# Expert blocks on one Trainium2 core: token rows kept as rounded values and rests, turned in the rounded type through three PSUM banks

## The reference, cut to what matters

```python
xb = h_pad[slot_tok].reshape(n_blocks, MOE_BLOCK, d)      # MOE_BLOCK = 128, d = 1024

def expert_block(args):
    xi, e = args
    return (jax.nn.silu(xi @ w_gate[e]) * (xi @ w_up[e])) @ w_down[e]   # 1024 -> 512 -> 1024

yb = lax.map(expert_block, (xb, block_expert)).reshape(n_blocks * MOE_BLOCK, d)
y = jax.ops.segment_sum(yb * slot_w[:, None].astype(yb.dtype), slot_tok, num_segments=n + 1)
```

## Time and profile before

| what | value |
|---|---|
| median of 3 runs | 4618.35 us (4615.28 to 4619.43) |
| the profiled execution's own time | 4615.54 us |
| its span in the profile | 4613.7 us |
| busy share of the span | PE 86%, PEld 63%, DVE 45%, ACT 34%, POOL 14% |
| mean granted clock of TensorE | 0.915 |
| DMA | 451.03 MB, mean 98 GB/s |

### The profile page before, as it was taken

How to read it: one execution, slowest core, us unless ns; L and a number is a source line. 1 busy time by engine, 2 the same in 40 slices (tenths; PEclk the granted TensorE clock), 3 DMA queues, 4 the chain that set the end, 5 groups by cost and what they waited for, 6 DMA issues and landing times. The chain is left out here.

```text
span 4613.7 us, 42989 instructions
## 1 busy us (share of the span) xinstructions
PE 3988.9 (86%) x16492; PEld 2886.4 (63%) x16492; DVE 2089.2 (45%) x2604; ACT 1548.8 (34%) x2420; POOL 652.5 (14%) x332
## 2 busy tenths in 40 slices
PE   6799789999799799995956899889999854999996
PEld 6587555558587355573735776567777744666664
DVE  0272366652381466722237413223442213666665
ACT  1312245541322354422141335321220112555552
POOL 0021200002021100020100011123333221110111
PEclk6799889998899799987988899999999966999997
DMA  4211100012121112231212111132333233999985
GB/s 157 72 37 39 35 14 28 28 33 82 64 51 35 25 55 60 64 105 46 39 45 45 41 30 14 28 87 73 82 96 71 75 112 111 355 352 356 354 295 218
DMA packets 354838, 451.03 MB, mean 98 GB/s; under 512 B 51981, under 2 KB 227266, under 8 KB 354130
## 3 DMA queue, kind: packets, MB, share of 16 engines
q1 hardware_dynamic: 341986, 423.11, 29.7%
q0 software_dynamic: 12656, 25.26, 1.5%
HBM read 408.39 MB, written 59.31 MB: 101 GB/s over the span
## 5 line engine op out<-in xcount | busy, mean ns | idle before, releaser
L1189 PE MATMUL values<-probs,vp 128*128 128x512 f32 x672 | 348.4, 600 | 12.0 <-issue 6.4
L1277 ACT ACTIVATE probs<-scores 128x512 f32<-128x512 f32 (+1 forms) x336 | 196.0, 583 | 306.3 <-PE scores L213 304.6
L211 PE MATMUL scores<-q_hi,k_rest 97*128 97x512 f32 (+1 forms) x336 | 262.2, 780 | 0.0
L3417 PE MATMUL dp<-h_t,abt 128*128 128x512 f32 x544 | 241.9, 597 | 1.1 <-ACT abt L3466 0.9
L3448 ACT ACTIVATE expert_hi<-wu 128x1024 fp32r<-128x1024 f32 x136 | 144.7, 1064 | 250.4 <-PE gp L213 250.4
L255 POOL TENSOR_TENSOR ring_r<-ring_w,ring_hi 128x1024 fp32r<-128x1024 f32 x44 | 116.7, 2654 | 758.7 <-ACT ring_hi L248 758.7
L1358 DVE TENSOR_REDUCE mx<-made 128x1 f32<-128x640 f32 (+1 forms) x272 | 203.7, 793 | 27.3 <-PE made L1130 26.5
L211 PE MATMUL smb<-x_t_r,merge_w_r 128*128 128x512 f32 x480 | 196.0, 408 | 19.1 <-POOL merge_w_r L2758 16.4
L211 PE MATMUL gates_ps<-x_t_r,ring_r 128*128 128x512 f32 (+1 forms) x560 | 206.2, 368 | 2.9 <-PEq L81 2.9
L779 DVE SCALAR_TENSOR_TENSOR conv_out<-conv_in,vectors,conv_out 128x1295 f32<-128x1295 f32 (+1 forms) x120 | 205.5, 1713 | 4.3
L212 PE MATMUL gates_ps<-h_t_r,ring_hi 128*128 128x512 f32 (+1 forms) x560 | 206.2, 368 | 0.0
(11 more groups left out here) (521 smaller groups left out, 9580.4 us busy)
## 6 DMA issues: line engine op xcount, KB each, us to landing
wg<-in_w_gate SPq DMA_DIRECT2D x34, 2048.0 KB, 9.7
wu<-in_w_up SPq DMA_DIRECT2D x34, 2048.0 KB, 11.0
h_t<-in_w_down SPq DMA_DIRECT2D x34, 2048.0 KB, 9.6
ahead_w<-in_w_ada SPq DMA_DIRECT2D x48, 512.0 KB, 3.9
ring_w<-in_w_in SPq DMA_DIRECT2D x44, 512.0 KB, 4.1
mod_w<-in_w_mod SPq DMA_DIRECT2D x12, 1024.0 KB, 5.3
x_kept<-x_t SPq DMA_DIRECT2D x6, 2048.0 KB, 12.0
ahead_w<-in_w_mod SPq DMA_DIRECT2D x24, 512.0 KB, 3.6
```

What stands on the lines that cost most here:

```text
L211: nc.tensor.matmul(out, lhs[1], rhs[0], start=start, stop=False, **kw)
L1189: nc.tensor.matmul(O[b % 2][:, 0:w], vp[g // 2 % 2][:, kb, g % 2 * VD:g % 2 * VD + P], pr[m % 3][:, 0:w], start=kb == 0, stop=kb == nk - 1 ...
L1277: nc.scalar.activation(pr[m % 3][:, 0:w], S[m % 2][:, 0:w], ACT.Exp, scale=scale).then_inc(s.exped, 1)
L3417: m = nc.tensor.matmul(dp[half][:, :], at[:, j, :], wd[u][:, j, half * 512:(half + 1) * 512], start=j == 0, stop=j == FK - 1)
```

## The change

`turn_out` writes each token row as 2048 values where it was 1024: the 1024 rounded values, then the 1024 rests. ACT's copy out of PSUM goes into a tile of the rounded type, and DVE, which had no part in this stage, subtracts it from the bank (L700 in the new file). A store is 1024 KB. A gather brings both parts of a row, 8 KB where it was 4 KB. `turn_x` has 16 transpositions, with data, identity and result in the rounded type, in four groups: the rounded values of features 0 to 511, their rests, the rounded values of features 512 to 1023, their rests. They go to three banks, so the fourth group takes the first group's bank again. ACT copies banks 0 and 2 to `x_hi`, DVE banks 1 and 0 to `x_rest`; DVE's part is a copy and no longer needs `x_hi`. The first gather buffer moves to a free part of the old h. The rounded identity is made by ACT at the start of the stage.

```diff
@@ turn_out @@
-    with ExitStack() as es, stage(nc, "turned copied out0 out1") as s, nc.Block() as block:
-        rows = [es.enter_context(sbuf(nc, f"to_rows{i}", [P, DK, P], F32)) for i in range(2)]
+    with ExitStack() as es, stage(nc, "turned rounded rest out0 out1") as s, nc.Block() as block:
+        rows = [es.enter_context(sbuf(nc, f"to_rows{i}", [P, 2, DK, P], F32R)) for i in range(2)]
...
                     if n >= 4:
-                        pe.wait_ge(s.copied, n - 3)
+                        pe.wait_ge(s.rest, n - 3)
...
                     act.wait_ge(s.turned, n + 1)
-                    nc.scalar.activation(rows[i % 2][:, 4 * h:4 * h + 4, :], ps[n % 4][:, :, :], ACT.Copy)\
-                        .then_inc(s.copied, 1)
+                    nc.scalar.activation(rows[i % 2][:, 0, 4 * h:4 * h + 4, :], ps[n % 4][:, :, :], ACT.Copy)\
+                        .then_inc(s.rounded, 1)
+
+        @block.vector
+        def _(dve):
+            for i in range(n_tiles):
+                if i >= 2:
+                    dve.wait_ge(stored[i % 2], 16 * (i // 2))
+                for h in range(2):
+                    n = 2 * i + h
+                    dve.wait_ge(s.rounded, n + 1)
+                    nc.vector.tensor_tensor(rows[i % 2][:, 1, 4 * h:4 * h + 4, :], ps[n % 4][:, :, :],
+                                            rows[i % 2][:, 0, 4 * h:4 * h + 4, :].bitcast(F32), ALU.subtract).then_inc(s.rest, 1)
...
-                sp.wait_ge(s.copied, 2 * (i + 1))
-                sp.dma_start(out[i * P:(i + 1) * P, :], rows[i % 2][:, :, :].rearrange("p c t -> p (c t)"))\
-                    .then_inc(stored[i % 2], 16)
+                sp.wait_ge(s.rest, 2 * (i + 1))
+                sp.dma_start(out[i * P:(i + 1) * P, :],
+                             rows[i % 2][:, :, :, :].rearrange("p a c t -> p (a c t)").bitcast(F32)).then_inc(stored[i % 2], 16)
@@ experts: tiles @@
-            xb = two("xb", [P, D])
+            xb1, xb1_r = es.enter_context(sbuf_views(nc, "xb1", [P, 2 * D]))
+            xb = [flat_h[:, 2 * FK * D:2 * FK * D + 2 * D], xb1]
+            xb_r = [k.h_r[:, :, :].rearrange("p a b -> p (a b)")[:, 2 * FK * D:2 * FK * D + 2 * D], xb1_r]
+            ident_r = sb("ident_r", [P, P], F32R)
...
-            xp = [es.enter_context(psum(nc, f"xp{i}", [P, 4, P], F32)) for i in range(2)]
+            xp = [es.enter_context(psum(nc, f"xp{i}", [P, 4, P], F32R)) for i in range(3)]
@@ experts: POOL (fixed blocks; the loop likewise) @@
-                        pool.wait_ge(s.xt_made, 2 * (b - 1))
+                        pool.wait_ge(s.xt_made, 4 * (b - 1))
@@ experts: PE @@
                 def turn_x(b, u):
                     pe.wait_ge(gathered[u], count(b, 8, 16 - 8 * u))
-                    for half in range(2):
-                        if later(b):
-                            pe.wait_ge(s.x_rest, count(b, 2, half - 1))
+                    for n in range(4):
+                        half, part = divmod(n, 2)
+                        if n == 3:
+                            pe.wait_ge(s.x_hi, count(b, 2, 1))
+                        elif later(b):
+                            pe.wait_ge(s.x_hi if n == 2 else s.x_rest, count(b, 2, 0))
                         for q in range(4):
-                            c = 4 * half + q
-                            m = nc.tensor.transpose(xp[half][:, q, :], xb[u][:, c * P:(c + 1) * P], k.ident)
+                            c = part * DK + 4 * half + q
+                            m = nc.tensor.transpose(xp[n % 3][:, q, :], xb_r[u][:, c * P:(c + 1) * P], ident_r[:, :])
                         m.then_inc(s.xt_made, 1)
 
                 def gate_up(b, u):
+                    pe.wait_ge(s.x_hi, count(b, 2, 2))
                     pe.wait_ge(s.x_rest, count(b, 2, 2))
...
+                pe.wait_ge(s.ident_made, 1)
                 turn_x((None, 0), 0)
@@ experts: ACT @@
                 def round_x(b):
                     for half in range(2):
-                        act.wait_ge(s.xt_made, count(b, 2, half + 1))
-                        nc.scalar.activation(x_hi[:, 4 * half:4 * half + 4, :], xp[half][:, :, :], ACT.Copy)\
+                        act.wait_ge(s.xt_made, count(b, 4, 2 * half + 1))
+                        nc.scalar.activation(x_hi[:, 4 * half:4 * half + 4, :], xp[2 * half][:, :, :], ACT.Copy)\
                             .then_inc(s.x_hi, 1)
...
+                nc.scalar.activation(ident_r[:, :], k.ident, ACT.Copy).then_inc(s.ident_made, 1)
                 round_x((None, 0))
@@ experts: DVE @@
                 def rest_x(b):
                     for half in range(2):
-                        dve.wait_ge(s.x_hi, count(b, 2, half + 1))
+                        dve.wait_ge(s.xt_made, count(b, 4, 2 * half + 2))
                         chunks = slice(4 * half, 4 * half + 4)
-                        nc.vector.tensor_tensor(x_rest[:, chunks, :], xp[half][:, :, :], x_hi[:, chunks, :].bitcast(F32),
-                                                ALU.subtract).then_inc(s.x_rest, 1)
+                        nc.vector.tensor_copy(x_rest[:, chunks, :], xp[1 - half][:, :, :]).then_inc(s.x_rest, 1)
@@ second_block @@
-    r.rows = nc.dram_tensor("token_rows", [SEQ, D], F32, kind="Internal").ap()
+    r.rows = nc.dram_tensor("token_rows", [SEQ, 2 * D], F32, kind="Internal").ap()
```

More of the change, by code:

```diff
@@ L3264, in turns_of @@
             return eng.value_load(r.block_expert[0:1, LOOPED:LOOPED + 1], min_val=1, max_val=LOOPED // 2)
-        names = ("table_in pad_set ids_copied down_in0 down_in1 gathered0 gathered1 xt_made x_hi x_rest w_hi w_rest "
+        names = ("table_in pad_set ident_made ids_copied down_in0 down_in1 gathered0 gathered1 xt_made x_hi x_rest w_hi w_rest "
                  "used silu_done mult_done a_made a_kept d_made d_kept stored0 stored1")
@@ L3359, in _ @@
                         u = 1 - c
-                        pool.wait_ge(s.xt_made, count(b, 2, -2))
+                        pool.wait_ge(s.xt_made, count(b, 4, -4))
                         listed(ix[u], 2 * i + (FIXED + 1 + c), 0)
```

## The result

| what | before | after |
|---|---|---|
| median us | 4618.89 (4615.28 to 4622.69, 4 runs) | 4679.11 (4676.32 to 4681.36, 4 runs) |
| profiled execution: own time, span | 4615.54, 4613.7 | 4678.95, 4677.1 |

A forecast was written before the change was run, and what follows sets the result against it. PE was taken to set the pace, the DMA engines only just keeping up. Blocks 24.4, `turn_out` 9.5, first gather 1.0, less 0.3, gave 34.6 us: 4650.1 against the profiled execution, 4653 against the median, range 4641 to 4668.

The forecast's parts named there:

- The fourth group waits, and `dp` behind it: In each expert block, the fourth group waits for ACT's first `x_hi` copy, starting 0.5 us later than `dp` does now.
- What one rounded transposition takes: On PE, 0.06 us each, so four add 0.24 and `dp` is delayed 0.74 us per block; 0.93 at 0.11 each.
- How often: The delay of `dp` counts 33 times, in blocks 1 to 29 and four of the loop: 24.4 us.
- Rival A: A rounded transposition takes 0.11 us, by its load or two passes: delays 30.7 us, total 4660; chance 0.28.
- DVE and ACT: In the blocks, two DVE subtractions become copies priced the same, and ACT's work stays the same: no cost.
- The DMA engines: In the blocks, the doubled gather needs 1.02 of the old block, 19.7 us, under PE's 20.08: no cost.
- Rival B: In the blocks, weights fall behind on the DMA engines: block some 20.5 us, total 4666; chance 0.07.
- `turn_out`: The stage that writes the token rows gets longer by 9.5 us, lower bound 6.5.
- the 2.9 to 3.0: Sign that the forecast is right: `turn_out`'s stores are 2.9 to 3.0 us apart.
- The first gather: PE waits 1.0 us longer for the first gather, less 0.3 gained turning the first rows at half clock.
- Rival C: In the blocks, the third bank hides the fourth group and `dp` does not move: 4625, not slower; chance 0.10.

The follow-up runs named there:

- e3_late: The changed kernel, with PE turning the fourth group between the two halves of the down product: 4666.49 us, ratio 1.0097 to the kernel before.
- f1_rows_only: The kernel before with the change's `turn_out` and 8 KB gathers, but PE turning only the rounded half of each row: 4629.20 us, ratio 1.002.
- g1_pad160: The kernel before with 160 unread identity transpositions added to PE's program where PE waits for the first gather: 4637.26 us, ratio 1.0037.
- g2_pad256: The kernel before with 256 unread identity transpositions added to PE's program where PE waits for the first gather: 4647.85 us, ratio 1.006.
- h1_short: The changed kernel with PE's loop entered three turns earlier, 504 matmuls fewer in PE's program, same work: 4647.94 us, ratio 1.0063 to the kernel before.
- f2_turned_twice: The kernel before with each of a block's 8 float32 transpositions made twice into the same place: 4659.32 us, ratio 1.0077.

## Why the prediction was right or wrong

1. **The fourth group waits, and `dp` behind it**: right, in every block. Its start was put 0.50 later than `dp`'s before; it is 1.78 - 1.31 = 0.47. Both ends of that difference were counted 0.1 too late (1.88 and 1.38 behind `ap`), which cancels. `e3_late` shows the wait by taking it away.
2. **What one rounded transposition takes** is the term that was mis-sized in the block. It was taken at 0.06 us and measured 0.088 within the twelve and 0.37/4 = 0.093 in the fourth group. So the delay is 0.47 + 0.37 = 0.84 and not 0.74. The step that failed here is the choice between the ends: I subtracted the one-column load's 83 ns from the turning load's 141, and took the 58 left for the distance of two starts. The changed kernel's rows have the same 141 for a load, and 88 between loads. A difference of two durations in a pipeline isn't its pace. The rule of the Trainium skill (TensorE: Matmul & The Clock Gate, section LDWEIGHTS (loading the stationary operand)), columns over 1.2, gives 107 ns for these loads. The measured 88 lies below it, and the 109 of float32 agrees.
3. **How often**: 33 x 0.84 = 27.7, and the blocks lost 30.9. The 28 blocks from one `ap` to the next lost 24.8 us, 0.89 each, since every second one is 0.10 longer than the delay explains. The first block gave 0.4 back. The loop and its exit took 6.5 more, of which 3.1 are the two falls of the granted clock; the sum had no term for those. Rival A's 30.7 for the blocks meets the size by luck: its price of 0.11 is not that of a rounded transposition (0.088), and the clock makes up for it.
4. **DVE and ACT** cost nothing: right, 687 ns against 686.
5. **The DMA engines** cost nothing: right. The margin was underrated: they were put at 102% of the old block, and `f1_rows_only` fits the doubled gather into a block of 19.36 us at 99.8% without a wait. The queue of the gathers took 3.1% more and not 3.75%. Rival B falls.
6. **`turn_out`**: 9.5 forecast, 9.5 measured, and 9.4 where it was made alone. The stores are 21.14 us from first to last issue, (21.14 - 0.32)/7 = 2.97 apart, as the 2.9 to 3.0 said. The landing is 1.3 longer, 3.9 against 2.6, for the 1.27 of the sum.
7. **The first gather**: 0.7 forecast, 1.3 measured.
8. **What had no term**: 21.0 us in stages that the change doesn't touch. This is the step that put the time outside the range: the sum was made from the engines' work in the two changed places, and put all else at nothing without a reason. `g1_pad160` and `g2_pad256` show the loss with nothing of the change but matmuls added to PE's program, not yet executed, and `h1_short` takes it away from the changed kernel by the length of the program alone. How the length acts stays open. With it the terms add up: 21.0 + 9.5 + 1.3 + 30.9 + 0.7 = 63.4.

Rival C (the third bank hides the fourth group) falls with the 0.84. The direction was right for its reasons. Between the two profiled executions 63.4 - 34.6 = 28.8 us were missed: 21.0 have this cause, 30.9 - 24.4 = 6.5 are the blocks', and the rest is small. Between the medians 25.6 were missed.

## What to carry to other kernels

A third bank doesn't free a queue when its fourth user still waits for the first: place the group that needs the freed bank behind independent work of the same engine (here between the halves of the down product, 12 to 15 us), and count every instruction added to the engine that bounds the stage at the pace between two starts, not at a difference of durations. Where a change adds or removes hundreds of written-out instructions, compare the stages that it doesn't touch before explaining those that it does, and try the same kernel with its loop entered a few turns earlier: here that alone was worth 27 us, though the gain didn't last when the program became shorter still. Compare the medians of several runs too: one profile of `f2_turned_twice` showed 24 us of such a loss, and its median 8.

## What the runs showed of the hardware

- The length of PE's program on this core changes the speed of DMA transfers that have nothing to do with it. With 160 matmuls more, placed behind the stretch measured, 133472 packets of 88.31 MB take 26.8% of it instead of 23.3%; 160 instructions more in ACT's program leave it at 23.2%. With 912 fewer in PE's they take 29.1%, so it has no simple order. Up to 2100 us the share doesn't move (0.16 in both kernels, 200 to 2100 us).
- Two starts of a 128-column transposition are 0.088 us apart in the rounded type and 0.109 in float32, while a single load takes 141 ns in both.
- With 99.8% of the DMA engines in use, the blocks' gate weights landed 3.2 us later and the block took 19.36 us where it had taken 19.34.
- Waits of PE of 2.44 and 1.92 us were followed by 3.5 us at a granted clock of 0.51 in the changed kernel, and by 1.00 in the kernel before, where they were 2.46 and 1.92 us.
